# A second attention on one core: the compressed part split over more steps, the end of the attention rearranged

## What is computed

```python
attn_out = nsa_attention(q, k_cmp, v_cmp, k_slc, vs, k_win, vw, gates)   # 8 heads of 64, 512 queries
# per block of queries: o = g0 * o_cmp + g1 * o_slc + g2 * o_win
#   o_cmp: masked softmax over 31 compressed keys; o_slc, o_win: softmax over the 512 keys up to the query
conv_out = short_conv_mixer(hc, cg, bg, conv_w)
mixed = concat([rms_norm(attn_out, g_out[:512]), rms_norm(conv_out, g_out[512:])])
x = x + mixed @ w_o
h = rms_norm(x, g_ffn_norm)
x = x + square(relu(h @ w_up)) @ w_down
```

## Time and profile before

| | |
|---|---|
| median of three runs | 1971.48 us (1966.75 to 1973.75) |
| profiled execution, its own time | 1966.23 us |
| its span, first to last instruction | 1964.9 us |
| TensorE busy | 1758.2 us (89%) |
| VectorE busy | 803.8 us (41%) |
| ScalarE busy | 560.5 us (29%) |
| GpSimd busy | 123.1 us (6%) |
| second attention and drain | about 1399 to 1546 us of the span |

### The profile page before, as it was taken

One profiled execution on the slowest core, in us unless ns is written; L12 is line 12 of the kernel. 1 busy time (PEld: TensorE's weight loads), 2 busy tenths in 40 slices (PEclk: granted clock), 3 DMA queues, 4 the chain that ended last, 5 costly groups with the idle time before them and its releaser, 6 DMA issues.

```text
span 1964.9 us, 20245 instructions
## 1 busy us (share of the span) xinstructions
PE 1758.2 (89%) x8127; PEld 1137.8 (58%) x8127; DVE 803.8 (41%) x1313; ACT 560.5 (29%) x983; POOL 123.1 (6%) x127
## 2 busy tenths in 40 slices
PE   5999899887999885998888888999888899999998
PEld 2656567556778652333333333687544578888786
DVE  2154755566433433111111112538566534444443
ACT  2224553554423331000000000431544442222221
POOL 0002021113000001000000000000100100011100
PEclk9999799987999886999999999999889899999999
DMA  8221201123512336999999999243400122223301
GB/s 302 94 65 43 86 22 65 44 89 126 151 57 95 150 150 263 423 423 425 424 423 424 424 424 416 83 152 86 129 1 1 44 86 86 86 86 106 109 1 44
DMA packets 92257, 329.39 MB, mean 168 GB/s; under 512 B 7428, under 2 KB 22404, under 8 KB 67588
## 3 DMA queue, kind: packets, MB, share of 16 engines
q1 hardware_dynamic: 85408, 315.80, 41.5%
q10 hardware_dynamic: 5412, 8.03, 1.2%
q0 software_dynamic: 1344, 4.25, 0.6%
HBM read 322.82 MB, written 4.19 MB: 166 GB/s over the span
## 4 chain that ended last, share of the span: by engine, by line
PE 71%; DMA 10%; DVE 10%; ACT 5%; issue 3%; ACTq 0%; SPq 0%; DVEq 0%
PE PS L658 21%; PE PS L776 11%; PE PS L1007 9%; PE PS L401 7%; DMA ring<-in_w_exp_gate_dram 4%; DMA room<-in_w_exp_gate_dram 4%; PE PS L397 3%; PE PS L532 3%; PE PS L787 3%; PE PS L614 2%; PE PS L842 2%; PE PS L457 1%; PE PS L679 1%; DMA ring<-in_w_in_dram 1%; PE PS L957 1%
## 5 line engine op out<-in xcount | busy, mean ns | idle before, releaser
L1717 DVE TENSOR_TENSOR wR<-ring,wR 128x1024 fp32r<-128x1024 f32 (+2 forms) x134 | 151.4, 1130 | 234.6 <-ACT wR L1120 234.5
L1120 ACT CAST wR<-ring 128x1024 fp32r<-128x1024 f32 (+2 forms) x134 | 130.0, 971 | 210.4 <-PE PS L1007 128.2
L1007 PE MATMUL PS<-wR,hR 128*128 128x512 f32 x768 | 177.8, 393 | 8.9 <-DVE tmp L2434 6.9
L658 PE MATMUL PS<-xR,wR 128*128 128x512 f32 x768 | 175.6, 390 | 0.0
L1007 PEld LDWEIGHTS PS<-wR,hR 128*128 128x128 f32 x768 | 144.7, 189 | 42.0 <-DVE tmp L2434 9.6
L658 PEld LDWEIGHTS PS<-xR,wR 128*128 128x128 f32 x768 | 144.0, 188 | 30.3 <-issue 0.4
L658 PE MATMUL PS<-hR,wR 128*128 128x512 f32 x528 | 132.0, 409 | 7.9 <-DVE hR L2415 3.3
L776 PE MATMUL PS<-room,xeT 128*64 128x512 f32 x512 | 115.0, 602 | 14.6 <-DMA room<-in_w_exp_gate_dram 14.6
L776 PE MATMUL PS<-ring,xeT 128*64 128x512 f32 x512 | 116.1, 607 | 13.1 <-DMA ring<-in_w_exp_gate_dram 12.4
L658 PEld LDWEIGHTS PS<-hR,wR 128*128 128x128 f32 x528 | 102.0, 195 | 36.2 <-issue 9.4
L658 PE MATMUL PS<-hR1h,wR 128*128 128x512 f32 x320 | 107.7, 409 | 8.3 <-DVE hR1m L2094 7.4
(11 more groups left out here) (423 smaller groups left out, 2665.5 us busy)
## 6 DMA issues: line engine op xcount, KB each, us to landing
ring<-in_w_exp_gate_dram SPq DMA_DIRECT2D x32, 1024.0 KB, 26.9
room<-in_w_exp_up_dram SPq DMA_DIRECT2D x32, 1024.0 KB, 26.5
ring<-in_w_exp_down_dram SPq DMA_DIRECT2D x32, 1024.0 KB, 26.7
room<-in_w_exp_gate_dram SPq DMA_DIRECT2D x32, 1024.0 KB, 27.4
ring<-in_w_exp_up_dram SPq DMA_DIRECT2D x32, 1024.0 KB, 26.9
room<-in_w_exp_down_dram SPq DMA_DIRECT2D x32, 1024.0 KB, 27.1
ring<-in_w_mod_dram SPq DMA_DIRECT2D x12, 2048.0 KB, 8.0
ring<-in_w_in_dram SPq DMA_DIRECT2D x11, 2048.0 KB, 8.7
```

What stands on the lines that cost most here:

```text
L658: mm = T.matmul(b, o[s][:, k, :], x(t, k), start=(k == ks[0] and j == 0), stop=(k == ks[-1] and j == 2))
L1007: mm = T.matmul(down[m], uR[:, r % 2, s, k, 128 * i:128 * i + 128], o[t][:, 0, 512 * q:512 * q + 512], start=(k + j == 0), stop=(k == 3 an ...
L1120: A.copy(parts(wR, chunks, n)[0], W.view(unit)[:, ks, cs]).then_inc(act_hi.sem, act_hi.up(key))
L1717: V.tensor_tensor(lo, W.view(unit)[:, ks, cs], hi.bitcast(F32), ALU.subtract) \
```

## The change

The two calls of the compressed part become five: `c_scores`, `c_exp` (ScalarE's exponential), `c_norm` (VectorE's norm), `c_turn` (TensorE's transposes), `c_put` (VectorE's copy to `cpT`), called at `m` = 3, 4, 5, 7, 8 for round 3 and at `m` = 9, 10, 11, 13, 14 (then every eight) for the others. A new call `drain(m)` at `m` = 32 and 33 brings the cast and subtraction of the conv tiles and of the first weight chunk into the attention's last steps. On ScalarE it also takes `rinv` of the three rounds done, as `Ln` and `Exp`; VectorE multiplies those 384 queries by it, and the 128 of round 0 after their own square root and reciprocal. GpSimd's four multiplies go. So that the new writes find free memory, tile `k` of the projection's input is kept at place `(k + 4) % 8` and the weight halves swap parity.

```diff
@@ parts
-        return [wR[:, n % 2, x, 0:a * b].rearrange("p (a b) -> p a b", b=b) for x in range(2)]
+        at = (n + (chunks is ffn_chunks)) % 2
+        return [wR[:, at, x, 0:a * b].rearrange("p (a b) -> p a b", b=b) for x in range(2)]
@@ select_order
-            if m < 32 and m % 8 == (3 if m < 8 else 1):
-                compressed1(sel_steps[m][0])
-            if m < 32 and m % 8 == (6 if m < 8 else 5):
-                compressed2(sel_steps[m][0])
+            for n, step in enumerate((c_scores, c_exp, c_norm, c_turn, c_put)):
+                at = (3, 4, 5, 7, 8)[n], (9, 10, 11, 13, 14)[n]
+                if m == at[0] or m >= at[1] and (m - at[1]) % 8 == 0 and m < 32:
+                    step(3 if m == at[0] else 3 - m // 8)
+            if m in (32, 33):
+                drain(m)
@@ ScalarE
             def values2(m):
                 i = sel_steps[m][0]
-                if i == 0:
-                    A.wait_ge(*dve_sel["tot", 1])
-                    A.activation(rinv[:, 128:512], rinv[:, 128:512], ACT.Sqrt).then_inc(s.sem, s.up(("rms2", 1)))
                 A.wait_ge(*pe_sel["o", i])
...
-                if i == 0:
-                    A.wait_ge(*s.last)
-                    A.wait_ge(*dve_sel["sc", 31])
-                    copy_hi(wR3, ffn_chunks, 0)
 
             def square2(i):
                 if i == 0:
-                    A.wait_ge(*dve_sel["tot", 0])
-                    A.activation(rinv[:, 0:128], rinv[:, 0:128], ACT.Sqrt).then_inc(s.sem, s.up(("rms2", 0)))
+                    A.wait_ge(*pe_sel["tot", 0])
+                    A.activation(rinv[:, 0:128], bank(("tot2", 0))[:, 0:128], ACT.Sqrt, bias=eps, scale=1.0 / 512) \
+                        .then_inc(s.sem, s.up(("rms2", 0)))
+
+            def drain(m):
+
+                if m == 32:
+                    A.wait_ge(*pe_sel["s", 31])
+                    A.wait_ge(*dve_sel["conv"])
+                    conv_hi((4, 5))
+                    A.wait_ge(*pe_sel["pT", 29, 1])
+                    copy_hi(wR3, ffn_chunks, 0)
+                else:
+                    conv_hi((6, 7))
+                    A.wait_ge(*dve_sel["tot", 1])
+                    A.activation(rinv[:, 128:512], rinv[:, 128:512], ACT.Ln).then_inc(s.sem, s.up())
+                    A.wait_ge(*s.last)
+                    A.activation(rinv[:, 128:512], rinv[:, 128:512], ACT.Exp, scale=-0.5).then_inc(s.sem, s.up("rinv1"))
@@ VectorE
             def values2(m):
                 i = sel_steps[m][0]
                 if i == 0:
-                    V.wait_ge(*act_sel["rms2", 1])
-                    V.reciprocal(rinv[:, 128:512], rinv[:, 128:512]).then_inc(s.sem, s.up())
+                    V.wait_ge(*act_sel["rinv1"])
+                    V.tensor_tensor(mixT[:, 0:4, 128:512], mixT[:, 0:4, 128:512],
+                                    rinv[:, 128:512].unsqueeze(1).broadcast_to([128, 4, 384]), ALU.mult).then_inc(s.sem, s.up())
...
+            def drain(m):
+                if m == 33:
                     sub_lo(wR3, ffn_chunks, 0)
-                    V.wait_ge(*act_sel["rms2", 0])
-                    V.reciprocal(rinv[:, 0:128], rinv[:, 0:128]).then_inc(s.sem, s.up("n2"))
+                for k in (4, 5) if m == 32 else (6, 7):
+                    V.wait_ge(*act_ffn["mR", k])
+                    V.tensor_tensor(hR3[:, 1, k - 4], mixT[:, k, :], hR3[:, 0, k - 4].bitcast(F32), ALU.subtract) \
+                        .then_inc(dve_ffn.sem, dve_ffn.up(("mR", k)))
@@ GpSimd
-        G.wait_ge(*dve_sel["n2"])
-        for j in range(4):
-            G.tensor_tensor(mixT[:, j, :], mixT[:, j, :], rinv, ALU.mult).then_inc(pool_ffn.sem, pool_ffn.up(("n2", j)))
```

More of the change, by code:

```diff
@@ L962, in square2 @@
             def square2(i):
-                b = pool.take(T, ("tot2", i), dve_sel["tot", i])
+                b = pool.take(T, ("tot2", i), dve_sel["tot", i] if i else act_sel["rms2", 0])
                 T.wait_ge(*act_sel["sqa", i])
@@ L967, in square2 @@
                 mm.then_inc(pe_sel.sem, pe_sel.up(("tot", i)))
-            select_order(scores, compress1, compress2, compress3, compressed1, compressed2, turn2, values2, square2)
+            select_order(scores, compress1, compress2, compress3, c_scores, lambda i: None, lambda i: None, c_turn,
+                         lambda i: None, lambda m: None, turn2, values2, square2)
         def ffn():
@@ L1076, in attention_order, with select_order @@
             yield
-    def select_order(scores, compress1, compress2, compress3, compressed1, compressed2, turn2, values2, square2):
+    def select_order(scores, compress1, compress2, compress3, c_scores, c_exp, c_norm, c_turn, c_put, drain, turn2, values2,
+                     square2):
         for m in range(36):
@@ L1589, in values2, with conv_hi @@
                 A.activation(sq[:, i % 2, :], bank(("o2", i)), ACT.Square).then_inc(s.sem, s.up(("sqa", i)))
-                if i == 0:
-                    A.wait_ge(*s.last)
-                    A.wait_ge(*dve_sel["sc", 31])
-                    copy_hi(wR3, ffn_chunks, 0)
             def square2(i):
                 if i == 0:
-                    A.wait_ge(*dve_sel["tot", 0])
-                    A.activation(rinv[:, 0:128], rinv[:, 0:128], ACT.Sqrt).then_inc(s.sem, s.up(("rms2", 0)))
-            select_order(scores, compress1, compress2, compress3, compressed1, lambda i: None, turn2, values2, square2)
+                    A.wait_ge(*pe_sel["tot", 0])
[14 more added lines that the diff above has]
+                    A.activation(rinv[:, 128:512], rinv[:, 128:512], ACT.Exp, scale=-0.5).then_inc(s.sem, s.up("rinv1"))
+            def conv_hi(ks):
+                for k in ks:
+                    A.copy(hR3[:, 0, k - 4], mixT[:, k, :]).then_inc(act_ffn.sem, act_ffn.up(("mR", k)))
+            select_order(scores, compress1, compress2, compress3, lambda i: None, c_exp, lambda i: None, lambda i: None,
+                         lambda i: None, drain, turn2, values2, square2)
         def ffn():
@@ L1607, in ffn @@
                 if n == 0:
-                    A.wait_ge(*dve_sel["conv"])
-                    for k in mix_tiles:
-                        if k < 4:
-                            A.wait_ge(*pool_ffn["n2", k])
-                        A.copy(hR3[:, 0, k], mixT[:, k, :]).then_inc(s.sem, s.up(("mR", k)))
+                    A.wait_ge(*dve_sel["n2"])
+                    for k in range(4):
+                        A.copy(hR3[:, 0, k + 4], mixT[:, k, :]).then_inc(s.sem, s.up(("mR", k)))
                     continue
@@ L2365, in compressed2, with c_put @@
                     .then_inc(s.sem, s.up(("cp", i)))
+            def c_put(i):
                 V.wait_ge(*pe_sel["cpT", i])
@@ L2412, in ffn @@
                 if n == 0:
-                    for k in mix_tiles:
+                    for k in range(4):
                         V.wait_ge(*act_ffn["mR", k])
-                        V.tensor_tensor(hR3[:, 1, k], mixT[:, k, :], hR3[:, 0, k].bitcast(F32), ALU.subtract) \
+                        V.tensor_tensor(hR3[:, 1, k + 4], mixT[:, k, :], hR3[:, 0, k + 4].bitcast(F32), ALU.subtract) \
                             .then_inc(s.sem, s.up(("mR", k)))
```

30 lines of the change are left out of this document (19 added, 11 removed).

## The result

The changed kernel takes 1957.64 us (median of 12 runs, 1950.47 to 1963.10). The kernel before, run beside it, takes 1970.58 us (12 runs, 1964.88 to 1976.26). The ratio is 0.9938, 95% interval [0.9925, 0.9951], that is 12.2 us less, between 9.7 and 14.8. Its profiled execution took 1956.09 us with a span of 1954.7 us, against 1966.23 and 1964.9.

What follows compares the result with a forecast made beforehand. No engine is full in the second attention; TensorE's once-per-round wait for `cp` costs twice. Rounds 8.8, drain 2.2 and 3.3 make 14.3 us at best, 6.8 at worst; about 9 with three of four clocks falling: 1961.5 us, range 1953 to 1967.5.

Steps and rivals of the forecast that it cites:

- the shorter wait that costs twice: Second attention: TensorE's 3.61 us wait for `cp` also slows the work behind it; about 1.7 us replaces it.
- The new wait in the rounds: TensorE, before a transpose of `q` or `p2b`: 1.6 to 2.1 us, released by VectorE's scaling, replacing the wait for `cp`.
- The size of the rounds: Second attention: rounds 3 to 1 gain 8.8 us at best, 3.1 at worst; round 0's transposes come 2.8 or 1.0 forward.
- its share of idle time: Rounds 3, 1 and 0: gain taken as 55% or 20% of VectorE's idle time, the shares worked out for round 2.
- So the low end weighs three quarters.: Rounds: the case of the clock falling behind the new waits outweighs that of it holding; six of eight similar waits fell.
- The clock at 0.50 after most of them: Sign in the changed profile: TensorE's clock at its lower level behind most of the new waits in the rounds.
- The transposes that want them wait for VectorE's step 14 anyway: Rounds: the `cpT` copy holds two of four pool banks until step 15, without delaying the transposes that want them.
- Slower: Rival, chance 0.04: low clock falls on the value products, 3.2 us each in rounds 3, 2 and 1; 1974 us.
- The drain: End of the attention: the step up to the Square gains 2.2 us at best, 0.4 at worst, then 3.3 more.
- 3.3 us from the Square on: Drain, Square to end of output tile 0: 10.7 us against 13.8; gain 3.1, or 3.3 with the clock's return inside.
- the Square waits 3 us for ScalarE's own list: Drain: casts, two table loads, `Ln` and `Exp` delay the Square after the products; TensorE idles 3 to 4 us.
- The subtractions: Drain, VectorE's attention tiles: 0.63 us each with GpSimd free, 1.22 kept for the range.

Runs made afterwards that it cites:

- e9_drain_fill: Changed kernel with the compressed part at its old steps and 24 needless identity transposes ahead of each wait for `cp`; 1957.10 us, ratio 0.9941 to the kernel before.
- e5_one_load: Changed kernel with a square root on ScalarE and reciprocal on VectorE in place of `Ln` and `Exp`; 1954.10 us, ratio 0.9923 to the kernel before.
- e2_drain: Changed kernel with the compressed part back at its old steps, only the drain rearranged; 1962.94 us, ratio 0.9971 to the kernel before.
- e6_after_fill: Changed kernel with 11 to 13 identity transposes ahead of the new wait for the scaling, once a round; 1954.07 us, ratio 0.9932 to the kernel before.
- e10_drain_fill_one: As `e9_drain_fill`, with a square root on ScalarE and reciprocal on VectorE in place of `Ln` and `Exp`; 1955.65 us, ratio 0.9940 to the kernel before.

## Why the prediction was right, and where it was off

Forecast 1961.5 us, range 1953 to 1967.5, faster with 0.78. Measured 1957.64: the sign, the range and both parts of the mechanism held, the shorter wait that costs twice and the rearranged drain. The size was 9 us, where the trace shows 10.5 and the runs 12.2 (9.7 to 14.8). That it came so near is partly luck: by its weights round 3 should have gained 1.3 us and gained 0.1, round 2 should have gained 1.9 and gained 3.8.

**The new wait in the rounds.** Right in place, size and releaser: "one of 1.6 to 2.1 us before a transpose of `q` or `p2b`". Measured 1.71, 1.59, 1.75 and, a little below the range, 1.46 us in round 0. The waits for `cp` went from 13.2 us to nothing.

**The size of the rounds.** Round 2 was worked out step by step as 3.7 us with the clock held and 1.3 with it down. It measured 3.8, held. Round 1 was given 2.6 or 0.9 by its share of idle time and measured 1.8, held. Round 3 was given 2.5 or 0.9 and measured 0.1. Round 0 was given 2.8 or 1.0 and measured 1.7. The sum of all four is 7.4 us, between the 11.6 at best and 4.1 at worst of the prediction.

**"So the low end weighs three quarters."** This weight failed, and with it the sign "The clock at 0.50 after most of them". It counted waits of 1.85 to 2.3 us elsewhere in the kernel and took their share for these. In the profiled execution the clock held through rounds 2 and 1, and fell in rounds 3 and 0. A share counted over the whole kernel, between waits with other work around them, did not carry over. With the two ends weighed equally the sum is 10.5 us, the number of the trace, though not round by round. In round 3 the clock did not fall behind the new wait (1433.12) but 9 us later, behind the one for the banks.

**The wait for the banks.** "The transposes that want them wait for VectorE's step 14 anyway" was wrong. They wait 1.2 to 1.4 us longer in each of rounds 3 to 1, because the copy of `cpT` stands behind that step on VectorE and takes 1.20 us itself. In round 2 it cost little on the path: 3.8 us gained, 3.7 predicted without it. In round 3 it is the last wait ahead of the fall of the clock. The rival "Slower" had named both parts, the waits ahead of steps 14 and 15 and the low clock on the value products, at 3.2 us per round. It happened in one round, round 3, at 2.2 us on the value products and 1.0 on the scores ahead of them, not in the two from which it was to decide. And it took the place of the 2.6 us behind the old wait, so the net loss was 0.6.

**The drain.** Predicted: 3.3 us from the Square on. Measured from the Square's start to the first addition to `xT`, 14.56 us before and 11.02 after: 3.5. Predicted: the Square waits 3 us for ScalarE's own list. Measured 0.5 us, and TensorE idle for 1.24 us where 3 to 4 were forecast, so this sign failed. The 3 us was the case of full speed in round 0; there the clock fell, and the products were held back. With the four matmuls with `cpT` at full speed (1.07 us instead of 1.97) `e9_drain_fill` shows 1.7 us. The eight behind them stayed at half speed there; at the pace of round 1 (eight in 1.94 us, here 3.47) they would end 1.5 us earlier, and the Square would be 3.2 us late, an estimate. So the list is as long as predicted (4.6 us from ScalarE's last copy to the Square, 4.7 predicted), and half speed on the products hid most of it. No pause showed at either load: `Ln` starts at 1524.64, when the load that began at 1523.35 ends. The Trainium skill ("ScalarE: Activation LUTs", What ACT_TABLE_LOAD costs) would have 1.38 us more at each; the trace again decides against it.

**The subtractions.** Predicted 0.63 us each once GpSimd is silent, 1.22 as the bound. Measured 0.684 us.

**What stays open.** Why the runs gained 12.2 us where the stretch gained 10.5 in the traces, which the interval allows. And what decides behind which of the short waits the clock falls, and how long it stays low: in the same order of round 3 it reads 0.52 from 1440 to 1450 in `e5_one_load` and 0.66 in the changed kernel. For the same reason the drain's size is less sure than its sign: 10.0, 10.2 and 11.5 us were measured with the same instructions in it (`e2_drain`, `e6_after_fill`, the changed kernel).

## What to carry to other kernels

When TensorE waits once per round in a stage where no engine is full, look at the durations right behind the wait before you count the wait: here holding the clock with 24 idle transposes gained as much (10.0 us) as reordering three engines did (7.5). If you shorten waits instead of filling them, don't count on the clock: behind the shorter waits of round 3 half speed cost 3.2 us, where behind the old one it cost 2.6. When you move work off one engine's list in a drain, write down the other engine's chain beside it: here a table load less ahead of the Square shortened TensorE's wait for it by 1.6 us and the drain by 0.2 (`e10_drain_fill_one`). And a wait that is gone from the list is not yet gained: count the waits that take its place.

## What the runs showed of the hardware

Waits of 1.2 to 1.75 us were followed by half speed in some rounds and not in others of the same execution, and with 24 transposes of a constant in place of the old waits the clock read 1.00 in every window up to 1520. The Trainium skill ("TensorE: Matmul & The Clock Gate", A second HAM failure mode: psum-queue depth-cycling) tells of a bf16 kernel with short idles between groups of matmuls that come so often that the clock goes up and down; the windows of 0.54 at 1442 and 1.00 from 1455 on agree with it.

VectorE's subtraction of two 128x512 operands takes 0.684 us alone and had a median of 1.216 us beside GpSimd's multiplies. The Trainium skill ("SBUF — State Buffer", 🔬 SBUF: two separate sides) says that a VectorE operation with two inputs in SBUF and a GpSimd operation that reads SBUF exclude each other. The eight subtractions before, 629 to 1762 ns, agree.

`Ln` followed by `Exp` took two table loads of 1.28 us. The Trainium skill ("ScalarE: Activation LUTs", 🔬 Table sets: the hidden batching unit) counts one load for this pair, since one set holds both. Here the program has two, at 1523.35 and 1525.18.
